# An expert layer's head: norm, turns and logits tile by tile, and its modulation rows loaded and combined one stage earlier

## The chip, the cores and the metric

One core of a Trainium2 chip runs the whole program, 68,690 instructions in a long row of stages. The metric is the device time of one execution in microseconds; the span of a profile runs from its first to its last instruction. The engines are TensorE (PE, with its weight loads PEld), VectorE (DVE), ScalarE (ACT), GpSimd (POOL) and SyncE (SP), which only issues DMAs.

## The reference, cut to what matters

Two transformer blocks, all in float32. The first block has two layers, each with a mixer and an expert layer. Of the first block:

```python
x = x + g1 * y
h = rms_norm(x, norm2_g[i]) * (1.0 + sc2) + sh2
x = x + g2 * expert_choice_ffn(h, moe_router[i], moe_w1[i], moe_w3[i], moe_w2[i])
if not last:
    ctx = ctx + cg1 * yc
    hc = rms_norm(ctx, norm2_g[i]) * (1.0 + csc2) + csh2
    ctx = ctx + cg2 * expert_choice_ffn(hc, moe_router[i], moe_w1[i], moe_w3[i], moe_w2[i])
```

`x` has 512 rows of 1024, `ctx` 256 rows. The shift `sh2`, the scale `sc2` and the gates `g1`, `g2` are rows of 1024 that come from a modulation of the condition (`mod_dram` in the kernel, six parts of 1024 for each of the two conditions). `expert_choice_ffn` computes a softmax over 16 experts from `h @ router`, lets each expert choose its 64 best rows of `x` (and 32 of `ctx`), and runs a gated network with weights of 3 x 4 MB for each expert.

## The kernel before, in words

Rows of `x` lie in SBUF as six tiles of 128 rows (four of `x`, two of `ctx`). The program is a row of stages; each (`Stage`, L29) has its own semaphores and a block in which every engine has its own list of instructions, written out by hand, and all engines meet at its end. No planner orders anything.

The last stage of each mixer is `add_gated` (L1624): `linear` (L412) multiplies the mixer's output with a 1024 x 1024 weight and adds it, times the gate, to `x`. The weight comes in four pieces of 256 columns and 1 MB, loaded by SP (L452) into a ring of 3 landing buffers in layer 0 and of 2 in layer 1. ScalarE makes the high part of a piece (L505) and of the rows tile by tile (L510), VectorE the low parts (L523, L530), TensorE does 24 matmuls a unit (one tile, 256 columns; L493), and VectorE multiplies with the gate and adds (L1636, L1637). Eight banks of accumulator let TensorE run ahead of VectorE by eight units. `linear` can already take a list `beside` of DMAs that GpSimd issues at the stage's start (L460).

The next stage is the expert layer, `mixture` (L1130). SP loads the gain row of the norm and, for one or two conditions, a scale and a shift row, each spread over 128 partitions (512 KB each; L1224 to L1227), then the router, then the first four quarters of expert weights (1 MB each). Meanwhile ScalarE squares and sums all tiles of `x` (L1382). VectorE waits for the rows, combines `(1 + scale) * norm gain` (L1450), waits for all sums, makes the mean (L1456), ScalarE the root (L1384), VectorE the inverse (L1458), and then the normed tile in two instructions (L1460, L1462). TensorE turns each tile with eight transposes (L1277), ScalarE copies the turned tile out (L1388), and SP stores the normed tile to DRAM for the later gathers (L1233). When all tiles are turned, TensorE does the logits, 8 float32 matmuls of 16 columns a tile (two records each in the profile, L1284). Then come the softmax, a ranking by rounds of eight on VectorE (L1475 to L1477), the gathers by indirect DMA, and the stream: 192 quarters of 1 MB go through four landing buffers, ScalarE's high part (L1364), VectorE's low part (L1426) and 12 matmuls each. A quarter beyond the fourth is loaded only when a low part has been made, and the first low part comes after the ranking on VectorE.

In layer 0 the expert layer has six tiles and two conditions, in layer 1 four tiles and one.

Of the kernel before, what the change touches and what calls it, by code (L numbers as in the profile page):

```python
# [13 lines left out]
P = 128  # L14
D = 1024
# [396 lines left out]
def linear(nc, h, K, w, jobs, RING=3, whole=None, low_from=None, beside=(), mod=None):  # L412
# [18 lines left out]
    with Stage(nc) as st:  # L431
# [84 lines left out]
        def _(dve):  # L516
# [18 lines left out]
            for c, piece in enumerate(pieces):  # L535
# [9 lines left out]
                lo_part(c + RING)  # L545

# [583 lines left out]
def mixture(nc, d, i, x, nt, mod_dram, cst):  # L1130
# [21 lines left out]
    with Stage(nc) as st:  # L1152
        land = [st.sb(f"w_quarter{c}", [P, QK, D]) for c in range(NL)]
# [3 lines left out]
        hid = st.sb("hidden", [P, D])  # L1157
        g2r = st.sb("row_gain", [R, D])
        shared = st.sb("gains_then_rows", [P, 4, D])
        gain, shift = shared[:, 0:2, :], shared[:, 2:4, :]  # L1160
        rows, ys = [shared[0:R, c, :] for c in range(2)], [shared[0:R, 2 + c, :] for c in range(2)]
        ng = hid
        rw = st.sb("router", [P, KD, E])
        ss, rs = (st.sb(n, [P, nt]) for n in ("sum_squares", "inverse_root"))
        junk = st.sb("squares", [P, D])
# [18 lines left out]
        consts = st.sem("gains_landed")  # L1184
        router_landed = st.sem("router_landed")
        g2_landed = st.sem("row_gain_landed")
        squared, mean_ready, root_ready = st.sem("squared"), st.sem("mean_ready"), st.sem("root_ready")
# [27 lines left out]
        def _(sp):  # L1215
# [8 lines left out]
            sp.dma_start(ng[:, :], d["norm2_g"][i].partition_broadcast(P)).then_inc(consts, 16)  # L1224
            for r in range(NROW):
                sp.dma_start(gain[:, r, :], mod_dram[r, 4 * D:5 * D].partition_broadcast(P)).then_inc(consts, 16)
                sp.dma_start(shift[:, r, :], mod_dram[r, 3 * D:4 * D].partition_broadcast(P)).then_inc(consts, 16)  # L1227
# [42 lines left out]
        def _(pe):  # L1270
            bank = (p3, py)
            for t in range(nt):
# [7 lines left out]
            pe.wait_ge(router_landed, 16)  # L1280
            for t in range(nt):
                pe.wait_ge(n_kept, 2 * t + 2)
                for k in range(KD):
                    mm = nc.tensor.matmul(pl[:, t, :], nT[:, k, t * P:(t + 1) * P], rw[:, k, :],  # L1284
                                          start=(k == 0), stop=(k == KD - 1), skip_group_check=True)
            mm.then_inc(scored, 1)
# [70 lines left out]
        def _(act):  # L1357
# [21 lines left out]
            for t in range(nt):  # L1379
                if t:  # L1380
                    act.wait_ge(squared, t)
                nc.scalar.activation(junk[:, :], x[:, t, :], ACT.Square, accum_out=ss[:, t:t + 1]).then_inc(squared, 1)  # L1382
            act.wait_ge(mean_ready, 1)
            nc.scalar.activation(rs[:, :], ss[:, :], ACT.Sqrt).then_inc(root_ready, 1)  # L1384
            for t in range(nt):
                for half in range(2):
# [3 lines left out]
                                         .rearrange("p (k r) -> p k r", k=HK), ACT.Copy).then_inc(n_kept, 1)  # L1390
            act.wait_ge(ready, 1)
# [25 lines left out]
        def _(dve):  # L1417
# [30 lines left out]
            dve.wait_ge(consts, 16 * (1 + 2 * NROW))  # L1448
            for r in range(NROW):
                last = nc.vector.scalar_tensor_tensor(out=gain[:, r, :], in0=gain[:, r, :], scalar=1.0, in1=ng[:, :],  # L1450
                                                      op0=ALU.add, op1=ALU.mult)
            chain(last)
            if RT > R:
                nc.vector.memset(hid[R:RT, :], 0.0)
            dve.wait_ge(squared, nt)
            nc.vector.tensor_scalar(ss[:, :], ss[:, :], 1.0 / D, EPS, ALU.mult, ALU.add).then_inc(mean_ready, 1)  # L1456
            dve.wait_ge(root_ready, 1)
            chain(nc.vector.reciprocal(rs[:, :], rs[:, :]))  # L1458
            for t in range(nt):
                chain(nc.vector.scalar_tensor_tensor(out=h[:, t, :], in0=x[:, t, :], scalar=rs[:, t:t + 1],  # L1460
# [871 lines left out]
NDR = 14  # L2332


def odd_layer(nc, d, x, modT, gates, gate_row, cst, ahead):

    ident = cst["ident"]
    RWI, NAD = 1920, 512
# [869 lines left out]
```

## Time and profile before

| | us |
|---|---|
| median of 3 runs (5191.65 to 5210.83) | 5204.43 |
| profiled execution | 5182.43 |
| its span | 5180.6 |
| PE busy | 4192.4 (81%) |
| DVE busy | 3071.3 (59%) |
| ACT busy | 1888.9 (36%) |
| mean granted TensorE clock | 0.879 of full speed |

The two expert layers are at 747 to about 1440 and at 2618 to about 3280 us of the span. In these stretches the core's 16 DMA engines move some 360 GB/s. A granted clock of 1.00 is 2.4 GHz, 0.50 is 1.2 GHz. In the timeline a row is one instruction or some merged ones: start, duration, engine, line, operation, output and input, and in brackets how long the engine sat idle before it and which instruction released it.

### The profile page before, as it was taken

To read this page: it belongs to the slowest core of one execution; us is meant where nothing else is said; L and a number is where in the kernel's file an instruction comes from. 1 tells how busy PE (TensorE), PEld (TensorE's weight loads), DVE (VectorE), ACT (ScalarE), POOL (GpSimd) and SP (SyncE) were. 2 spreads that over 40 slices of the span, in tenths; PEclk is the share of its full clock that TensorE was granted. 3 is DMA by queue.
4 is the path that set the end of the run, shared out by engine and by line. 5 is a ranking of instruction groups with operands and counts; after the bars stand their busy time and mean duration, and the time that the engine had idled before them with its cause. 6 is when DMAs were issued, how large, how long until landed. Compare 5 with 4: busy or idle time off the path is not lost. (4 is left out here: it accounts for less than half of the span.)

```text
span 5180.6 us, 68690 instructions
## 1 busy us (share of the span) xinstructions
PE 4192.4 (81%) x28028; PEld 3310.1 (64%) x28028; DVE 3071.3 (59%) x4349; ACT 1888.9 (36%) x2461; POOL 549.9 (11%) x419
## 2 busy tenths in 40 slices
PE   6868867999956887979669999686799856785998
PEld 2755665666656866869545555465687655674777
DVE  5259946888824556665458888436476234454672
ACT  4122324666622313222126666315322112352221
POOL 0111000111112003323001112002000001000000
PEclk9988787999978997978779999888899967897999
DMA  6120036999930220000249999400122201000322
GB/s 235 54 83 25 1 108 226 364 363 362 334 117 29 74 84 6 3 6 2 100 161 356 365 362 357 159 25 1 56 95 94 92 29 34 1 1 33 114 94 77
DMA packets 246407, 658.34 MB, mean 127 GB/s; under 512 B 27028, under 2 KB 91796, under 8 KB 245576
## 3 DMA queue, kind: packets, MB, share of 16 engines
q1 hardware_dynamic: 227808, 615.14, 33.3%
q0 software_dynamic: 8064, 30.46, 2.2%
q10 hardware_dynamic: 10224, 8.36, 0.5%
q8 instruction: 224, 3.67, 0.3%
q14 instruction: 87, 0.71, 0.0%
HBM read 624.97 MB, written 28.41 MB: 126 GB/s over the span
## 5 line engine op out<-in xcount | busy, mean ns | idle before, releaser
L1426 DVE TENSOR_TENSOR w_lo<-w_quarter,w_hi 128x2048 fp32r<-128x2048 f32 x384 | 874.0, 2287 | 200.0 <-ACT w_hi L1364 198.7
L1364 ACT ACTIVATE w_hi<-w_quarter 128x2048 fp32r<-128x2048 f32 x384 | 735.4, 1917 | 379.2 <-DMA w_quarter<-in_moe_w 188.3
L2682 DVE TENSOR_TENSOR w_lo<-w_chunks,w_hi 128x1024 fp32r<-128x1024 f32 x132 | 161.8, 1226 | 301.4 <-ACT w_hi L2660 301.4
L2634 PE MATMUL ffn_ps<-ffn_inT_hi,w_hi 128*128 128x512 f32 x704 | 276.4, 393 | 16.5 <-DVE w_lo L2682 16.5
L2634 PE MATMUL ffn_ps<-ffn_inT_lo,w_hi 128*128 128x512 f32 x704 | 275.9, 392 | 0.0
L2634 PE MATMUL ffn_ps<-ffn_inT_hi,w_lo 128*128 128x512 f32 x704 | 275.6, 391 | 0.0
L1265 POOL DMA_INDIRECT summed_dram<-gains_then_rows,row_token x32 | 137.9, 4310 | 1005.6 <-DVE gains_then_rows L1445 1005.6
L1312 PE MATMUL down_ps<-w_hi,hiddenT 128*96 128x512 f32 (+1 forms) x512 | 208.1, 406 | 39.2 <-DVE w_lo L1426 26.6
L900 PE MATMUL probT_ps<-ident,prob 128*128 128x128 f32 x896 | 164.6, 301 | 82.6 <-ACT prob L980 80.4
L967 ACT ACTIVATE probT<-probT_ps 128x256 f32<-128x256 f32 (+4 forms) x272 | 142.2, 523 | 223.5 <-PE probT_ps L900 223.5
L1312 PE MATMUL gate_ps<-w_hi,rowsT 128*96 128x512 f32 (+1 forms) x512 | 206.2, 403 | 12.5 <-DVE w_lo L1426 9.6
L1312 PE MATMUL up_ps<-w_hi,rowsT 128*96 128x512 f32 (+1 forms) x512 | 204.7, 400 | 7.4 <-DVE w_lo L1426 7.4
L2660 ACT ACTIVATE w_hi<-w_chunks 128x1024 fp32r<-128x1024 f32 x132 | 138.5, 1049 | 189.4 <-PE ffn_ps L2647 163.7
L1314 PE MATMUL gate_ps<-w_lo,rowsT 128*96 128x512 f32 (+1 forms) x512 | 204.4, 399 | 0.0
L1314 PE MATMUL down_ps<-w_lo,hiddenT 128*96 128x512 f32 (+1 forms) x512 | 204.2, 399 | 0.0
L1314 PE MATMUL up_ps<-w_lo,rowsT 128*96 128x512 f32 (+1 forms) x512 | 201.8, 394 | 0.0
L980 ACT ACTIVATE prob<-score_ps,negmax 128x256 f32<-128x256 f32 (+4 forms) x272 | 166.1, 611 | 87.2 <-DVE negmax L949 85.2
L588 PE MATMUL lin_ps<-w_hi,haT 128*128 128x512 f32 (+1 forms) x576 | 178.8, 391 | 23.3 <-DVE w_lo L612 23.3
L406 PE MATMUL turn_ps<-ident,normed 128*128 128x128 f32 x286 | 58.1, 377 | 166.1 <-DVE normed L363 153.5
L505 ACT ACTIVATE w_hi<-w_landing 128x2048 fp32r<-128x2048 f32 (+4 forms) x39 | 64.7, 1661 | 343.5 <-PE lin_ps L493 221.8
L900 PEld LDWEIGHTS probT_ps<-ident,prob 128*128 128x128 f32 x896 | 106.4, 150 | 126.2 <-ACT prob L980 118.3
L612 DVE TENSOR_TENSOR w_lo<-w_landing,w_hi 128x2048 fp32r<-128x2048 f32 (+2 forms) x28 | 56.2, 2007 | 184.4 <-ACT w_hi L602 184.4
(648 smaller groups left out, 10173.8 us busy)
## 6 DMA issues: line engine op xcount, KB each, us to landing
w_quarter<-in_moe_w SPq DMA_DIRECT2D x384, 1024.0 KB, 6.5
w_chunks<-in_f_w_up SPq DMA_DIRECT2D x88, 512.0 KB, 3.2
ada_landing<-in_ada_w SPq DMA_DIRECT2D x24, 1024.0 KB, 7.0
ada_ring<-in_ada_w SPq DMA_DIRECT2D x24, 1024.0 KB, 5.2
w_chunks<-in_f_w_down SPq DMA_DIRECT2D x44, 512.0 KB, 3.2
w_landing<-in_od_w_in SPq DMA_DIRECT2D x13, 1024.0 KB, 7.2
w_landing<-in_a_w_in SPq DMA_DIRECT2D x12, 1024.0 KB, 5.1
w_landing<-in_ev_w_in SPq DMA_DIRECT2D x6, 1024.0 KB, 7.4
```

The lines of the kernel that those rows point to most:

```text
L588: mm = nc.tensor.matmul(ps[n % 2][i][:, 0:width], h[:, g * HK + k, cols], v[:, c % NP, k, 0:width], start=(g + k + j == 0), stop=(g == 1 a ...
L900: mm = nc.tensor.transpose(tps(a, b), pr[:, i % SB, a:b], ident)
L967: nc.scalar.activation(pT[:, i % SB, 0:n], tps(0, n), ACT.Copy).then_inc(tkept, 1)
L980: nc.scalar.activation(pr[:, i % SB, 0:u[1]], score(i, 0, u[1]), ACT.Exp, bias=mx[:, m:m + 1], scale=scale, accum_out=sm[:, m:m + 1]).then ...
L1265: nc.gpsimd.indirect_dma_start(out=sum_dram, out_offset=bass.IndirectOffsetOnAxis(ap=idx[:, e:e + 1], axis=0), in_=ys[e % 2], in_offset=No ...
L1312: nc.tensor.matmul(out[0:R, cols], v[0][:, k, :], wh[c][:, kk, cols], start=first, stop=False, skip_group_check=True)
L1314: nc.tensor.matmul(out[0:R, cols], v[0][:, k, :], wl[c][:, kk, cols], start=False, stop=False, skip_group_check=True)
L1364: nc.scalar.activation(wh[g % NP][:, :, :], land[g % NL][:, :, :], ACT.Copy).then_inc(hi_ready, 1)
L1426: tt(wl[g % NP][:, :, :], land[g % NL][:, :, :], wh[g % NP][:, :, :].bitcast(F32), ALU.subtract) \
L2634: mm = nc.tensor.matmul(ps[c % 4][:, :], w[:, c % NP, cols], h[:, k, :], start=(k + i == 0), stop=(k == KD - 1 and i == 2))
L2660: nc.scalar.activation(wh[:, c % NP, :], land[:, c % NL, :], ACT.Copy).then_inc(hi_ready, 1)
L2682: nc.vector.tensor_tensor(wl[:, c % NP, :], land[:, c % NL, :], wh[:, c % NP, :].bitcast(F32), ALU.subtract).then_inc(split, 1)
```

## The change

`mixture` no longer loads and combines the rows. A new class `RowGains` holds them in SBUF, at a place that the stage before and the expert layer both leave free; `add_gated` passes its loads to `linear` as `beside` (GpSimd issues them) and its `combine` as `then`, which VectorE runs after the second weight piece's units. In layer 1 the ring of `linear` is 3 now, as in layer 0. In `mixture`, each tile has its own square, root, inverse and norm; the mean and the epsilon are folded into the root; the logits of tile t come on TensorE after the turn of tile t + 1. The landing buffers of the stream lie in another order in SBUF, around the rows.

```diff
-def linear(nc, h, K, w, jobs, RING=3, whole=None, low_from=None, beside=(), mod=None):
+def linear(nc, h, K, w, jobs, RING=3, whole=None, low_from=None, beside=(), mod=None, then=None):
...
                 lo_part(c + RING)
+                if c == 1 and then is not None:
+                    dve.wait_ge(beside_done, 16 * len(beside))
+                    then()
...
+class RowGains:
+    def __init__(self, nc, ctx, d, i, rows, mod_dram):
+        self.nc, self.rows = nc, rows
+        self.shared = ctx.enter_context(nc.sbuf_tensor(f"gains_then_rows_{Stage.turn}", [P, 4, D], F32))
+        self.hid = ctx.enter_context(nc.sbuf_tensor(f"gain_then_hidden_{Stage.turn}", [P, D], F32))
+        self.gain, self.shift = self.shared[:, 0:2, :], self.shared[:, 2:4, :]
+        self.loads = [(self.hid[:, :], d["norm2_g"][i].partition_broadcast(P))]
+        for r in range(rows):
+            self.loads.append((self.gain[:, r, :], mod_dram[r, 4 * D:5 * D].partition_broadcast(P)))
+            self.loads.append((self.shift[:, r, :], mod_dram[r, 3 * D:4 * D].partition_broadcast(P)))
+    def combine(self):
+        for r in range(self.rows):
+            self.nc.vector.scalar_tensor_tensor(out=self.gain[:, r, :], in0=self.gain[:, r, :], scalar=1.0,
+                                                in1=self.hid[:, :], op0=ALU.add, op1=ALU.mult)
...
-        land = [st.sb(f"w_quarter{c}", [P, QK, D]) for c in range(NL)]
+        land = [st.sb(f"w_quarter{c}", [P, QK, D]) for c in range(nt // 2)]
+        st.sb("gains_of_the_stage_before", [P, 5, D])
+        land += [st.sb(f"w_quarter{c}", [P, QK, D]) for c in range(nt // 2, NL)]
...
-            sp.dma_start(ng[:, :], d["norm2_g"][i].partition_broadcast(P)).then_inc(consts, 16)
-            for r in range(NROW):
-                sp.dma_start(gain[:, r, :], mod_dram[r, 4 * D:5 * D].partition_broadcast(P)).then_inc(consts, 16)
-                sp.dma_start(shift[:, r, :], mod_dram[r, 3 * D:4 * D].partition_broadcast(P)).then_inc(consts, 16)
...
+            def logits(t):
+                if t == 0:
+                    pe.wait_ge(router_landed, 16)
+                pe.wait_ge(n_kept, 2 * t + 2)
+                for k in range(KD):
+                    mm = nc.tensor.matmul(pl[:, t, :], nT[:, k, t * P:(t + 1) * P], rw[:, k, :],
+                                          start=(k == 0), stop=(k == KD - 1), skip_group_check=True)
+                return mm
...
-            pe.wait_ge(router_landed, 16)
-            for t in range(nt):
-                pe.wait_ge(n_kept, 2 * t + 2)
...
+                if t:
+                    logits(t - 1)
+            logits(nt - 1).then_inc(scored, 1)
...
-            for t in range(nt):
+            def root(t):
                 if t:
                     act.wait_ge(squared, t)
                 nc.scalar.activation(junk[:, :], x[:, t, :], ACT.Square, accum_out=ss[:, t:t + 1]).then_inc(squared, 1)
-            act.wait_ge(mean_ready, 1)
-            nc.scalar.activation(rs[:, :], ss[:, :], ACT.Sqrt).then_inc(root_ready, 1)
+                act.wait_ge(squared, t + 1)
+                nc.scalar.activation(rs[:, t:t + 1], ss[:, t:t + 1], ACT.Sqrt, bias=eps[:, :], scale=1.0 / D) \
+                    .then_inc(root_ready, 1)
+            act.wait_ge(eps_ready, 1)
+            for t in range(min(3, nt)):
+                root(t)
...
+                if t + 3 < nt:
+                    root(t + 3)
...
-            dve.wait_ge(consts, 16 * (1 + 2 * NROW))
-            for r in range(NROW):
-                last = nc.vector.scalar_tensor_tensor(out=gain[:, r, :], in0=gain[:, r, :], scalar=1.0, in1=ng[:, :],
-                                                      op0=ALU.add, op1=ALU.mult)
-            chain(last)
+            nc.vector.memset(eps[:, :], EPS).then_inc(eps_ready, 1)
...
-            dve.wait_ge(squared, nt)
-            nc.vector.tensor_scalar(ss[:, :], ss[:, :], 1.0 / D, EPS, ALU.mult, ALU.add).then_inc(mean_ready, 1)
-            dve.wait_ge(root_ready, 1)
-            chain(nc.vector.reciprocal(rs[:, :], rs[:, :]))
             for t in range(nt):
+                dve.wait_ge(root_ready, t + 1)
+                chain(nc.vector.reciprocal(rs[:, t:t + 1], rs[:, t:t + 1]))
...
+        gains = RowGains(nc, ctx, d, 0, 2, mod_dram)
+        add_gated(nc, catT, KD, d["ev_w_out"], x, list(range(NT)), lambda t: gates[:, 0 if t < LT else 1, :], gains.loads,
+                  gains.combine)
...
-        linear(nc, (hh, hl), K, w, [("tok", 0, D, tiles, keep)], RING=3 if n == TOK else 2, whole=inT)
+        linear(nc, (hh, hl), K, w, [("tok", 0, D, tiles, keep)], whole=inT, beside=beside, then=then)
...
+        ctx.close()
+        gains = RowGains(nc, outer, d, 1, 1, mod_dram)
+        add_gated(nc, catT, KD, d["od_w_out"], x, tiles[:LT], lambda t: gates[:, 0, :], gains.loads, gains.combine)
```

## Rows read from the trace of the kernel before

**Rows 1.** Windows: us, then each engine busy, PEclk, DMA share, GB/s; ranking, stream.
```profile
795.00:829.90 34.90, 3.30 (x16) 2.13 (x16) 31.27 (x74) 6.66 (x6) 3.88 (x3) 0.50 0.16 48
...
930.00:1030.00 100.00, 96.19 (x439) 66.80 (x437) 85.94 (x51) 67.79 (x46) 19.03 (x6) 1.00 1.01 362
```

**Rows 2.** Timeline of the first expert layer's head.
```profile
747.07 1.06 ACT L1382 ACTIVATE squares<-x 128x1024 f32<-128x1024 f32 x1 [51.10 <-PEq L67]
...
748.04 0.19 ACT L1382 ACTIVATION_READ_ACCUMULATOR squares<-x 128x1 f32 x1
...
754.14 1.28 ACT L1384 ACT_TABLE_LOAD   x1
757.82 2.36 DVE L1450 SCALAR_TENSOR_TENSOR gains_then_rows<-gains_then_rows,hidden 128x1024 f32<-128x1024 f32 x2 [11.10 <-DMA gains_then_rows<-mod_rows]
...
760.41 0.21 ACT L1384 ACTIVATE inverse_root<-sum_squares 128x6 f32<-128x6 f32 x1 [4.99 <-DVE sum_squares L1456]
760.65 0.19 DVE L1458 RECIPROCAL inverse_root<-inverse_root 128x6 f32<-128x6 f32 x1 [0.27 <-ACT inverse_root L1384]
760.88 1.28 DVE L1460 SCALAR_TENSOR_TENSOR normed_rows<-x,inverse_root,gains_then_rows 128x1024 f32<-128x1024 f32 x1
...
763.34 1.28 DVE L1460 SCALAR_TENSOR_TENSOR normed_rows<-x,inverse_root,gains_then_rows 128x1024 f32<-128x1024 f32 x1
...
763.48 1.97 PE L1277 MATMUL up_ps<-ident,normed_rows 128*128 128x128 f32 x8 [17.68 <-DVE normed_rows L1462]
...
777.51 17.39 PE L1284 MATMUL misc_ps<-router,normedT 128*128 128x16 f32 x96
...
794.94 0.26 DVE L1464 TENSOR_REDUCE row_max<-misc_ps 128x6 f32<-128x96 f32 x1 [19.24 <-PE misc_ps L1284]
```

**Rows 3.** Timeline of the second expert layer's head.
```profile
2618.08 1.06 ACT L1382 ACTIVATE squares<-x 128x1024 f32<-128x1024 f32 x1 [22.30 <-PEq L67]
...
2630.77 1.97 PE L1277 MATMUL up_ps<-ident,normed_rows 128*128 128x128 f32 x8 [13.97 <-DVE normed_rows L1462]
...
2639.89 13.68 PE L1284 MATMUL misc_ps<-router,normedT 128*128 128x16 f32 x64
```

**Rows 4.** Windows, PE alone: us, busy, PEclk, DMA share, GB/s; turns and logits.
```profile
768.30:769.50 1.20, 1.09 (x8) 1.00 1.00 406
...
777.50:780.00 2.50, 2.50 (x25) 0.98 0.97 231
...
2640.00:2642.00 2.00, 2.00 (x12) 0.50 0.91 307
```

**Rows 5.** Timeline: VectorE's keep in the stage ahead of the first expert layer.
```profile
742.96 0.42 DVE L1636 TENSOR_TENSOR gated<-lin_ps,gates 128x256 f32<-128x256 f32 x1 [2.00 <-PE lin_ps L493]
```

**Rows 6.** Timeline: the first weight piece of four stages, issue and first use.
```profile
663.77 10.09 SPq L452 DMA_DIRECT2D w_landing<-in_ev_w_out  x4
669.24 1.91 ACT L505 ACTIVATE w_hi<-w_landing 128x2048 fp32r<-128x2048 f32 x1 [11.68 <-DMA w_landing<-in_ev_w_out]
...
1485.12 18.72 SPq L452 DMA_DIRECT2D w_landing<-in_od_w_in  x4
...
1492.38 1.91 ACT L505 ACTIVATE w_hi<-w_landing 128x2048 fp32r<-128x2048 f32 x1 [13.38 <-DMA w_landing<-in_od_w_in]
...
1748.49 21.39 SPq L452 DMA_DIRECT2D w_landing<-in_od_w_in  x4
1749.09 4.32 POOL L459 DMA_DIRECT2D h1T_low_1b<-h1T_low  x8 [113.61 <-POOLq L67]
1755.17 1.91 ACT L505 ACTIVATE w_hi<-w_landing 128x2048 fp32r<-128x2048 f32 x1 [12.66 <-DMA w_landing<-in_od_w_in]
...
2557.72 16.67 SPq L452 DMA_DIRECT2D w_landing<-in_od_w_out  x4
...
2563.01 1.91 ACT L505 ACTIVATE w_hi<-w_landing 128x2048 fp32r<-128x2048 f32 x1 [8.63 <-DMA w_landing<-in_od_w_out]
```

**Rows 7.** DMA issues: line, engine, count, KB each, median us from issue to landing.
```profile
gates<-mod_rows POOLq DMA_DIRECT2D x2, 512.0 KB, 7.5
```

More of the change, by code:

```diff
@@ L1156, in mixture @@
         hT = [st.sb(f"hiddenT{c}", [P, KD, R], F32R) for c in range(2)]
-        hid = st.sb("hidden", [P, D])
+        hid, shared, gain, shift = gains.hid, gains.shared, gains.gain, gains.shift
         g2r = st.sb("row_gain", [R, D])
-        shared = st.sb("gains_then_rows", [P, 4, D])
-        gain, shift = shared[:, 0:2, :], shared[:, 2:4, :]
         rows, ys = [shared[0:R, c, :] for c in range(2)], [shared[0:R, 2 + c, :] for c in range(2)]
-        ng = hid
         rw = st.sb("router", [P, KD, E])
         ss, rs = (st.sb(n, [P, nt]) for n in ("sum_squares", "inverse_root"))
+        eps = st.sb("eps", [P, 1])
         junk = st.sb("squares", [P, D])
@@ L1519, with even_layer @@
 CONV = 512
-def even_layer(nc, d, x, modT, gates, cst, ahead, next_loads):
+def even_layer(nc, d, x, modT, gates, cst, mod_dram, ahead, next_loads):
     ident = cst["ident"]
@@ L1620, in even_layer, with add_gated @@
                       for ts in (range(LT), range(LT, NT)) for k in range(4)], ident)
-        add_gated(nc, catT, KD, d["ev_w_out"], x, list(range(NT)), lambda t: gates[:, 0 if t < LT else 1, :])
-def add_gated(nc, inT, K, w, x, tiles, gate):
+        gains = RowGains(nc, ctx, d, 0, 2, mod_dram)
+        add_gated(nc, catT, KD, d["ev_w_out"], x, list(range(NT)), lambda t: gates[:, 0 if t < LT else 1, :], gains.loads,
+                  gains.combine)
+        return gains
+def add_gated(nc, inT, K, w, x, tiles, gate, beside, then):
     n = inT.shape[2]
@@ L2332, with odd_layer @@
 NDR = 14
-def odd_layer(nc, d, x, modT, gates, gate_row, cst, ahead):
+def odd_layer(nc, d, x, modT, gates, cst, mod_dram, ahead):
     ident = cst["ident"]
@@ L2339, in odd_layer @@
     tiles = list(range(NT))
-    with ExitStack() as ctx:
+    with ExitStack() as outer, ExitStack() as ctx:
         def sb(name, shape, c=ctx):
             return c.enter_context(nc.sbuf_tensor(name, shape, F32))
-        catT = sb("mixedT_1", [P, KD, SEQ])
+        catT = sb("mixedT_1", [P, KD, SEQ], outer)
         gm = sb("gm1_1", [P, 2, KD])
@@ L2448, in odd_layer @@
             load_all(nc, [(gn[:, 0, :], d["gn_g"].partition_broadcast(P)), (gn[:, 1, :], d["gn_b"].partition_broadcast(P)),
[L2449 removed]
+                          (x[:, 0:LT, :], x_kept), (gates[:, 0, :], mod_dram[0, 2 * D:3 * D].partition_broadcast(P))], mod=mod)
             group_norm_gate(nc, Y, T, d, gn[:, 0, :], gn[:, 1, :], catT, ident, mod)
[L2451 removed]
+        ctx.close()
+        gains = RowGains(nc, outer, d, 1, 1, mod_dram)
+        add_gated(nc, catT, KD, d["od_w_out"], x, tiles[:LT], lambda t: gates[:, 0, :], gains.loads, gains.combine)
+        return gains
 F_TILES = 2816 // P
@@ L3104, in build @@
                        needed, loads)
-            even_layer(nc, d, x, modT[0], gates, cst, ahead, columns)
-            mixture(nc, d, 0, x, NT, mod_dram[0], cst)
+            gains = even_layer(nc, d, x, modT[0], gates, cst, mod_dram[0], ahead, columns)
+            mixture(nc, d, 0, x, NT, mod_dram[0], cst, gains)
         with nc.sbuf_tensor("gates1", [P, 1, D], F32) as gates:
-            odd_layer(nc, d, x, modT[1], gates, mod_dram[1][0, 2 * D:3 * D], cst, ahead)
-            mixture(nc, d, 1, x, LT, mod_dram[1], cst)
+            gains = odd_layer(nc, d, x, modT[1], gates, cst, mod_dram[1], ahead)
+            mixture(nc, d, 1, x, LT, mod_dram[1], cst, gains)
         forgetting(nc, d, x, cst)
```

12 lines of the change are left out of this document (3 added, 9 removed).

## The prediction

> **What bounds the kernel now.** I read first what is alike all over: in the stream of expert weights (windows by stage) TensorE is busy 96% of the time and the DMA engines are full [rows 1], so nothing outside that stream is worth anything unless it moves the stream's start. Then the head of each expert layer, which is the part that the change touches. It is a chain, and the timeline shows it as one [rows 2]: at 747.07 ScalarE squares six tiles, loads a table and is done at 755.42; VectorE meanwhile waits for the five row loads until 757.82, combines for 2.36 us, then scales the sums, waits for the root (until 760.62), inverts, and makes tile 0 between 760.88 and 763.48, where TensorE first moves. So the last wait to end ahead of tile 0 is that for the loads, and the squares of all tiles are behind it by 2.4 us. From 763.48 VectorE sets the pace (2.46 us a tile, the pitch from 760.88 to 763.34), TensorE turns each tile and waits. From 777.51 to 794.90 TensorE does the 96 matmuls of the logits alone, and VectorE starts again at 794.94, at once. What follows (softmax, ranking, gather, rows turned, 794.9 to 829.9) has VectorE busy for 31.3 of 34.9 us [rows 1]; none of it is touched, and the weight stream hangs on its end. The head of the second expert layer is the same with four tiles [rows 3]: 2618.08 to 2630.77 without TensorE, logits from 2639.89 to 2653.57.
>
> **Granted clock in the logits.** This decides the size [rows 4]. The clock is at 2.4 GHz (1.00) in the third tile's turn, where eight transposes take 1.09 us, and at 1.2 GHz (0.50) for most others, where they take 1.97 us. In the logits it is 0.98 for the first 2.5 us and 0.50 afterwards, though TensorE has no gap at all. In the second layer it is 0.50 already in the window from 2640 to 2642 (12 instructions in 2 us), right after a turn, and all 64 logit matmuls take 13.68 us [rows 3], 0.214 us each. [...]
>
> **The change part by part.**
>
> Start of tile 0, first layer. Removed from the path: the wait for the loads, 2.36 us of combining, five of six squares. Left: the memset of eps and ScalarE's wait for it (no such row; between 0 and 0.3 us, by the inverse, an instruction on six columns that is 0.23 us from start to start; I take 0.15), square and read 1.24, a self-wait 0.05, the table load 1.28, root 0.21, inverse until the product starts 0.26, product and sum until TensorE starts 2.60 (760.88 to 763.48) [rows 2]. 747.07 + 5.79 = 752.9: 10.6 us earlier. Second layer: the same without a table load (the function table is already the right one there, no such row stands in its head): 2618.08 + 4.5 = 2622.6 against 2630.77 [rows 3], 8.2 us earlier. VectorE's memset of the hidden rows lies beside ScalarE's square.
>
> The Trainium skill (ScalarE: Activation LUTs, "What ACT_TABLE_LOAD costs") gives such a load 1.28 us and a drain of about 1.4 us more. The load's own row agrees; the drain would be new on the path here, and by the page the gain below would be 1.4 us smaller.
>
> The tiles. VectorE now also inverts per tile: 2.46 + 0.23 (L1458's start to L1460's, 760.65 to 760.88) = 2.69 us a tile [rows 2]. ScalarE has per tile square, root and two copies, 1.24 + 0.05 + 0.21 + 1.2 = 2.7 us. TensorE has per tile a turn and 16 logit matmuls. At 1.2 GHz that is 1.97 + 16 x 0.214 = 5.39 us, twice VectorE's pace, so TensorE becomes the bound from tile 1 on. Order: turn 0, wait for tile 1, turn 1, logits 0, turn 2, ..., logits 5. First layer: tile 1 is ready at 752.9 + 2.69 = 755.6, then 5 x 1.97 + 6 x 3.42 = 30.4, end 786.0. Before 794.9: 8.9 us gained, less than the 10.6 of the start: from first turn to last logit TensorE needs 33.1 us at 1.2 GHz, and it needs 31.4 now, because the gaps of its turns are paid back by turns and logits that are in part at 2.4 GHz. Second layer: 2622.6 + 2.69 + 3 x 1.97 + 4 x 3.42 = 2644.9 against 2653.57: 8.7 us. Together 17.6. Ends: if no transposes and no logits lift the clock, this; if all of it ran at 2.4 GHz a tile would cost 1.09 + 16 x 0.107 (25 instructions stand in the first 2.5 us of the logits [rows 4]; I take 0.107) = 2.8 us, see the rivals.
>
> After the logits nothing changes. The table load for the exponential is issued after the last copy and hides under logits 5 (3.4 us) as it now hides under all of them. The stores of the normed tiles go out earlier; they must be in when the ranking is over, some 27 us after the logits. The DMA order in the SP queue: five loads fewer stand ahead of the router and the four weight quarters. Nobody waits for either in those 10 us but logits 0, for the router (64 KB), first needed at 757.6, ten microseconds after its issue, where a first piece of 1 MB takes five and a half [rows 6]. The eps bias costs an operand and no time that a row shows; below nothing is excluded, above I allow 0.1 us.
>
> The stage before (`linear` with `beside` and `then`). Moved there: five loads of 512 KB for layer 0 and three for layer 1, issued by GpSimd at the stage's start, and three combinations of 1.2 us on VectorE. The combinations come after the second of four weight pieces. TensorE needs 2.88 us a unit (VectorE's pair of 0.42 and 0.42 us and 2.00 idle [rows 5]), so VectorE has two thirds free, and eight units of accumulator lie between them: 2.4 us is hidden. If the loads were late there, VectorE would stand in front of the keeps, and TensorE would stop after 8 units, 23 us; the loads are by then 30 us old. The loads are not free. They meet the first weight piece, and on that hang its high part, its low part, the rows' split and TensorE's start, all in series. Piece 0 is used 5.47 us after its issue in this stage now (663.77 to 669.24) and 5.29 us in the second (2557.72 to 2563.01). The stages with loads beside them stand as nearest rows: 6.68 us with eight loads of 384 KB (1748.49 to 1755.17) and 7.26 us with two of 3 and 2 MB (1485.12 to 1492.38) [rows 6]. So 1.3 to 1.9 us more each; I take 1.5, nearer the row with many medium loads, 3.0 for both. Ends: 0 (GpSimd issues after SP), and, if piece 0 had to let all of it by at the 362 GB/s of the weight stream [rows 1], 2.6 MB + 1.6 MB = 7.2 + 4.3 = 11.5 us. Pieces 1 and 2 come later by up to 7 us, but are needed 17 us after piece 0. Ring 3 in place of 2 in the second layer puts one more low part (2.3 us) ahead of VectorE's first keep; the same eight units hide it, and TensorE had no gap between pieces there before, so it gains nothing either.
>
> The other buffer order in SBUF: 0, no row bears on it.
>
> Sum: 17.6 - 3.0 = 14.6 us. The profiled execution took 5182.4 us (span 5180.6 and 1.8 around it), that is 5167.8 after. The runs shown have a median of 5204.4, 22 us over that execution, and spread over 19 us; the same difference from the median gives 5189.8.
>
> **The rivals.**
>
> A. The clock goes up. TensorE has no gap from tile 1 on, and turns come among the logits. Then a tile costs 2.8 us, nearly VectorE's 2.69: first layer end 752.9 + 2.69 + 5 x 2.8 + 1.7 = 771.3 or so, 23.6 us gained, second 2622.6 + 2.69 + 3 x 2.8 + 1.7 = 2635.4, 18.2 gained, together 41.8 - 3.0 = 38.8: 5165.6. For it: two turns, 0.7 us apart, stand ahead of logits 0, and two came ahead of the third tile, the fast one [rows 4]. Against: 15 us of gapless logits at 0.50, and the window after the turn in the second layer. In part (one fast stretch a layer) it is worth some 2 to 4 us. The Trainium skill (TensorE: Matmul & The Clock Gate, "What's actually happening") has activity release the throttle; taken at its word the gapless stretch would be at 2.4 GHz, and this rival is what it gives. The logits of the trace go against it.
>
> B. The change does not pay in the start what it says: the overlap of squares, roots and copies on ScalarE makes tile after tile late (ScalarE at 2.7 us a tile and waits of both neighbours in it). Then TensorE waits at each tile. Price 1 to 1.5 us a tile, 10 to 15 us in all, result 0 to 5 us gained: 5202. Against: TensorE needs 5.4 us a tile, twice what ScalarE does.
>
> C. Slower: the GpSimd-issued row loads hold up the first weight piece. Two such loads, 1 MB, landed 7.5 us (median) after their issues where they met a stream [rows 7]; with 0.6 us between the issues that is 8.1 us, 130 GB/s. At that pace 2.6 MB take 20 us and 1.6 MB 12 us; if piece 0 stood behind them, TensorE would start 32 us late, and the result is 17.6 - 32 = 14 us slower, 5219. It turns to a loss from 17.6 us of delay in both stages together. For: TensorE's start has nothing ahead of it but this piece. Against: in the two nearest stages the piece was 1.3 and 1.9 us late only.
>
> **How the numbers follow.** Forecast 0.66, A 0.10 (in full or for the most part), B 0.14, C 0.05; 0.05 is left for what the spread does by itself. What a measurement of this kernel can tell from no change is about 0.5%, 26 us; the forecast lies inside. Faster by over 26 us needs A, or the forecast with a lucky median (the runs shown are up to 13 us off theirs): 0.19. Slower by over 26 us needs C at its worst and noise: 0.04. Within: 0.77. Range: from A's 5166, short of it by some, to B with noise: 5170 to 5210.
>
> **What would show it right or wrong.** TensorE's first transpose 5.8 us after the head's first square in layer 0 and 4.5 in layer 1; logits' end 38.9 and 26.8 us after that square (now 47.8 and 35.5); granted clock 0.50 there; the ranking part unchanged at 27 to 35 us; the first piece of the two stages before used 6.8 to 7 us after its issue; no wait of VectorE on the loads in it. The prediction is wrong if the clock in the logits is near 1.00, if TensorE waits between tiles for VectorE, or if the first piece is over 3 us late.

## The result, and the profile after

| kernel | median us (range, executions) | kernel before beside it | ratio, 95% interval |
|---|---|---|---|
| changed, first comparison | 5163.0 (5151.0 to 5191.0, 7) | 5203.2 (5184.4 to 5210.8, 7) | 0.9939 [0.9913, 0.9965] |
| changed, second comparison | 5166.8 (5161.9 to 5175.7, 6) | 5188.6 (5177.3 to 5211.0, 28) | 0.9963 [0.995, 0.9975] |

The change makes the kernel faster by some 0.4 to 0.6%: on either side of the 0.5% that the prediction took for its bound of no change. The forecast, 14.6 us off 5204.4, is a ratio of 0.9972: inside the second interval, just outside the first. As a time, 5189.8 was 27 and 23 us too high, and both medians lie under the range, by 7 and 3 us.

The profiled executions alone would tell the opposite: a span of 5180.6 us before and 5189.0 after. The unchanged recurrence of the second layer makes the difference. The rows are the timeline of SP, which loads a small matrix at the start of each of its two directions, and a window of the first direction (us; PE, PEld, DVE, ACT, POOL busy; clock, DMA share, GB/s); first the kernel before, then the changed one.

```profile
1950.83 0.35 SPq L2153 DMA_DIRECT2D w<-in_rw_w  x1
...
2220.61 0.33 SPq L2153 DMA_DIRECT2D w<-in_rw_w  x1
...
1951.00:2220.00 269.00, 233.70 (x4384) 212.06 (x4384) 160.13 (x302) 70.44 (x164) 88.63 (x90) 0.84 0.02 4
```
```profile
1950.73 0.35 SPq L2182 DMA_DIRECT2D w<-in_rw_w  x1
...
2237.39 0.33 SPq L2182 DMA_DIRECT2D w<-in_rw_w  x1
...
1951.00:2237.00 286.00, 250.46 (x4384) 228.79 (x4384) 160.43 (x303) 70.36 (x164) 88.65 (x90) 0.78 0.02 4
```

Start to start, the first direction took 269.8 us before and 286.7 after; in other profiles of the same two kernels it is the other way round, 283.9 before and 270.3 after. The swing goes with TensorE's granted clock: the same 4384 matmuls keep it busy for 233.7 us where the clock is 0.84 and for 250.5 us where it is 0.78, while VectorE, ScalarE and GpSimd are busy for the same time in both. So the kernel has to be read by stage, with times counted from where the change starts.

The head of the first expert layer in the changed kernel, timeline of all engines (start, duration, engine and line, operation, tiles; idle time before and what ended it in brackets), answering to [rows 2]:

```profile
749.61 1.06 ACT L1407 ACTIVATE squares<-x 128x1024 f32<-128x1024 f32 x1 [51.26 <-DVE eps L1480]
...
750.78 1.28 ACT L1409 ACT_TABLE_LOAD   x1
752.07 0.29 ACT L1409 ACTIVATE inverse_root<-sum_squares,eps 128x1 f32<-128x1 f32 x1
...
755.20 1.97 PE L1306 MATMUL up_ps<-ident,normed_rows 128*128 128x128 f32 x8 [7.03 <-DVE normed_rows L1488]
755.25 1.28 DVE L1486 SCALAR_TENSOR_TENSOR normed_rows<-x,inverse_root,gains_then_rows 128x1024 f32<-128x1024 f32 x1
...
757.85 1.97 PE L1306 MATMUL down_ps<-ident,normed_rows 128*128 128x128 f32 x8 [0.69 <-DVE normed_rows L1488]
757.91 1.29 DVE L1486 SCALAR_TENSOR_TENSOR normed_rows<-x,inverse_root,gains_then_rows 128x1024 f32<-128x1024 f32 x1
...
759.61 3.43 PE L1297 MATMUL misc_ps<-router,normedT 128*128 128x16 f32 x16
...
762.89 1.95 PE L1306 MATMUL up_ps<-ident,normed_rows 128*128 128x128 f32 x8
...
786.55 0.26 DVE L1490 TENSOR_REDUCE row_max<-misc_ps 128x6 f32<-128x96 f32 x1 [16.95 <-PE misc_ps L1297]
```

TensorE starts 5.6 us after the first square and has no gap from 759.61 until VectorE takes the logits 36.9 us after that square; before it was 16.4 and 47.9 us [rows 2]. The second layer, answering to [rows 3], and the granted clock of both stretches (windows: us, PE, PEld, DVE, ACT, POOL busy, clock, DMA share, GB/s):

```profile
2633.39 1.06 ACT L1407 ACTIVATE squares<-x 128x1024 f32<-128x1024 f32 x1 [33.98 <-DVE eps L1480]
...
2637.70 1.97 PE L1306 MATMUL up_ps<-ident,normed_rows 128*128 128x128 f32 x8 [5.75 <-DVE normed_rows L1488]
...
2659.03 0.22 DVE L1490 TENSOR_REDUCE row_max<-misc_ps 128x4 f32<-128x64 f32 x1 [13.42 <-PE misc_ps L1297]
```
```profile
766.00:786.00 20.00, 20.00 (x97) 20.00 (x97) 2.67 (x3) 5.66 (x10) 0.00 (x0) 0.50 0.68 264
2637.00:2659.00 22.00, 20.60 (x96) 20.09 (x96) 8.40 (x10) 7.85 (x15) 0.00 (x0) 0.50 0.94 370
```

The stage before, with the row loads in it (SP issues the weight pieces, GpSimd the rows), answering to [rows 6]; the second piece's high part is the fifth line, the combine the sixth:

```profile
666.44 12.21 SPq L453 DMA_DIRECT2D w_landing<-in_ev_w_out  x4
667.12 0.61 POOL L462 DMA_DIRECT2D gain_then_hidden<-in_norm_g  x1 [245.33 <-POOLq L67]
667.74 2.13 POOL L462 DMA_DIRECT2D gains_then_rows<-mod_rows  x4
671.67 1.91 ACT L506 ACTIVATE w_hi<-w_landing 128x2048 fp32r<-128x2048 f32 x1 [11.56 <-DMA w_landing<-in_ev_w_out]
682.17 1.92 ACT L506 ACTIVATE w_hi<-w_landing 128x2048 fp32r<-128x2048 f32 x1 [2.91 <-DMA w_landing<-in_ev_w_out]
...
714.45 2.35 DVE L1149 SCALAR_TENSOR_TENSOR gains_then_rows<-gains_then_rows,gain_then_hidden 128x1024 f32<-128x1024 f32 x2
...
2572.14 2.65 SPq L453 DMA_DIRECT2D w_landing<-in_od_w_out  x3
...
2577.55 1.91 ACT L506 ACTIVATE w_hi<-w_landing 128x2048 fp32r<-128x2048 f32 x1 [8.44 <-DMA w_landing<-in_od_w_out]
```

The first piece is used 5.23 and 5.41 us after its issue, against 5.47 and 5.29 before: no delay reaches it. The rows' bytes are paid by the second and third pieces. In layer 0 ScalarE takes them 15.7 and 19.7 us after the stage's first load and waits for both, where before it took them at 13.0 and 14.8 without a wait. TensorE shows no wait after its start, so this costs nothing.

**One table for all runs.** Each row is one profiled execution. "Linear" is from the first load of the residual stage to the head's first load; "head" from there to the release of the first buffer of the weight stream (its last instruction before that is VectorE's first low part); "to expert" from the same start to the first expert matmul. All in us, layer 0 / layer 1.

| kernel | linear | head | to expert |
|---|---|---|---|
| before | 83.3 / 60.3 | 77.6 / 58.6 | 82.9 / 67.7 |
| before, again (5203.6, one time) | 83.1 / 60.4 | 77.6 / 58.6 | 83.0 / 66.9 |
| changed | 83.0 / 61.1 | 66.5 / 48.9 | 76.0 / 57.3 |
| changed, again | 83.2 / 60.8 | 66.5 / 48.9 | 76.4 / 57.2 |
| logits_last | 83.9 / 60.5 | 70.7 / 51.0 | 80.1 / 59.5 |
| rows_early_only | 84.0 / 60.6 | 75.4 / 50.8 | 84.6 / 59.7 |
| rows_late | 83.5 / 59.7 | 76.5 / 56.3 | 85.9 / 64.6 |
| rows_sp_first | 92.9 / 65.0 | 66.5 / 48.9 | 76.0 / 57.8 |
| tile_moving | 83.2 / 60.1 | 56.8 / 44.3 | 66.1 / 53.0 |
| gather_first | 83.2 / 60.8 | 67.0 / 49.3 | 72.3 / 54.4 |
| tile_moving_gather_first | 83.2 / 59.9 | 57.3 / 44.7 | 62.7 / 49.8 |

The heads gain 11.1 and 9.7 us, 20.8 in all, more than the 17.6 forecast. But layer 0's expert matmuls start only 6.9 us earlier (82.9 to 76.0): 4.1 us are given back between the release of the stream and its first matmul. Layer 1 keeps 10.5 (9.7 against the other profile of before). Together that is 17.4 us (16.3 by the second profile of each kernel), and the two linear stages together cost 0.4 to 0.5. The weight streams add nothing: from the first expert matmul to the last scatter they take 604.0 and 608.1 us in the two profiles of before, 608.7 and 608.8 after (layer 1: 595.5 and 596.0, then 592.5 and 595.3).

### The profile page after: what moved, and what is told of

It is laid out like the page before. It is cut to its first block and busy times, and to the rows that moved or that the text cites. A ratio compares the mean times of both kernels' runs of the same rounds, so it can differ in the third digit from the quotient of the medians.

```text
span 5189.0 us, 68706 instructions
## 1 busy us (share of the span) xinstructions
PE 4220.5 (81%) x28028; PEld 3339.6 (64%) x28028; DVE 3075.9 (59%) x4357; ACT 1892.2 (36%) x2469; POOL 519.2 (10%) x427
## 5 line engine op out<-in xcount | busy, mean ns | idle before, releaser
L1337 PE MATMUL up_ps<-w_hi,rowsT 128*96 128x512 f32 (+1 forms) x512 | 204.4, 399 | 15.9 <-DVE w_lo L1458 15.8
L1284 POOL DMA_INDIRECT summed_dram<-gains_then_rows,row_token x32 | 105.3, 3291 | 1043.4 <-DVE gains_then_rows L1477 1043.4
```

Source lines behind the costliest of these rows:

```text
L1284: nc.gpsimd.indirect_dma_start(out=sum_dram, out_offset=bass.IndirectOffsetOnAxis(ap=idx[:, e:e + 1], axis=0), in_=ys[e % 2], in_offset=No ...
L1337: nc.tensor.matmul(out[0:R, cols], v[0][:, k, :], wh[c][:, kk, cols], start=first, stop=False, skip_group_check=True)
```

## The experiments

**The same kernel again, and its tile order taken back.** `after_again` is the changed kernel unedited:

> The changed kernel once more, nothing edited. In the two profiles so far the two expert heads (first SP instruction of the stage to the first released weight quarter) take 77.6 and 58.6 us before, 66.5 and 48.9 us after, 20.8 us less together; the medians of seven runs differ by 40 us. Theory 1 (the gain is in the heads alone, the rest is spread of stages that the change doesn't touch): the heads take 66.5 and 48.9 us again to 0.5 us, the weight streams and the stages between them differ from both profiles by up to 17 us with either sign, and the ratio comes out near 0.996 (20 us). Theory 2 (something beyond the heads is faster too, the streams for instance, which start earlier): the streams take clearly less than the 613 and 608 us of before, and the ratio stays at 0.994 or below.

It gave 0.9963, in agreement with theory 1, and the same heads to 0.1 us. `logits_last` leaves everything but the place of the logits:

```diff
-                if t:
-                    logits(t - 1)
+            for t in range(nt - 1):
+                logits(t)
             logits(nt - 1).then_inc(scored, 1)
```

> The changed kernel with the logits of all tiles after the turns of all tiles. Theory 1 (interleaving fills TensorE's gaps while the clock is at 1.2 GHz either way): turns at VectorE's pace of 2.66 us a tile, then 96 and 64 logit matmuls at 0.214 us; the heads are longer than in the changed kernel by 1.3 to 4.5 us (layer 0, less if the clock is at 2.4 GHz in the first logits as it was before) and 2.3 us (layer 1). Rival (interleaving is worth nothing, as the clock gives back the gaps): the heads equal those of the changed kernel to 0.5 us.

Measured 5178.5 us (5171.4 to 5202.6, 10), ratio 0.9992 [0.9976, 1.0008]; the heads are 4.2 and 2.1 us longer. Its TensorE has one turn per 2.65 us, waiting 0.69 us before each, and then all logits in one row:

```profile
772.57 20.50 PE L1297 MATMUL misc_ps<-router,normedT 128*128 128x16 f32 x96
```

So the logits between the turns fill TensorE's waits, and are worth 6.3 us of the heads' 20.8.

**The two halves of the change alone.** `rows_early_only` has the rows loaded and combined in the stage before, but squares, root and logits as before (one root after all squares, logits after all turns). `rows_late` has the new tile order, with the rows loaded and combined in the head again:

```diff
+            for to, src in gains.loads:
+                sp.dma_start(to, src).then_inc(consts, 16)
             sp.dma_start(rw[:, :, :], d["moe_router"][i]
...
+            dve.wait_ge(consts, 16 * len(gains.loads))
+            for r in range(gains.rows):
+                last = nc.vector.scalar_tensor_tensor(out=gain[:, r, :], in0=gain[:, r, :], scalar=1.0,
+                                                      in1=hid[:, :], op0=ALU.add, op1=ALU.mult)
```

> The rows are loaded and combined in the stage before, but the head squares all tiles, makes one mean and one root, turns all tiles, then does all logits, as before. Theory 1: the head now waits for the squares, done 4.8 us (layer 0, 755.4 against 760.2) and 4.7 us (layer 1) before the combination was; the heads take 72.8 and 53.9 us, 9.5 us less together, ratio 0.998. Rival (early rows are worth nothing without the tile order, or cost the stage before 3 us as predicted): heads as said, but the two stages before longer by 1.5 us each.

> Tile by tile norms and logits between the turns as in the changed kernel, but the rows are loaded by SP at the head's start and combined there as before. Theory 1: the tile order alone gains next to nothing, since tile 0 waits for the combination again: TensorE's first turn 0.5 to 1 us earlier than before, heads 76 to 77 and 57 us. Rival (the order of turns and logits is what gains): heads 72 or less and 55 or less.

Measured: `rows_early_only` 5185.6 us (5167.6 to 5206.6, 10), ratio 0.9997 [0.998, 1.0015], heads 75.4 and 50.8; `rows_late` 5185.3 us (5176.2 to 5197.9, 10), ratio 0.9996 [0.9981, 1.0011], heads 76.5 and 56.3. Neither half alone moves the time by what can be measured, though in the heads they are worth 10.0 and 3.4 us of the 20.8; the other 7.4 come only with both. The heads show why: with the loads in the path the tile order gains only 1.1 and 2.3 us, since tile 0 waits for the loads whatever the squares do (first turn 764.54, 15.6 us after its first square at 748.94); with the loads out of the way but six squares ahead of tile 0, the head gains 2.2 and 7.8 us. The last two numbers were expected at 4.8 and 4.7. The logits of `rows_early_only` in TensorE's timeline, and windows of it in layer 1 (us, PE busy, clock, DMA share, GB/s), show what came between:

```profile
775.68 20.50 PE L1296 MATMUL misc_ps<-router,normedT 128*128 128x16 f32 x96
...
2635.31 10.80 PE L1296 MATMUL misc_ps<-router,normedT 128*128 128x16 f32 x64
```
```profile
2635.30:2640.00 4.70, 4.70 (x39) 0.83 1.01 385
2640.00:2646.00 6.00, 6.00 (x29) 0.50 0.47 193
```

The same 96 matmuls took 17.39 us in the kernel before [rows 2] and take 20.50 here, and the 64 of layer 1 took 13.68 [rows 3] and take 10.80. In layer 1 the clock is still up for most of the first 4.7 us of the logits; in layer 0 all of them run at 0.50. How long the clock stays up behind the turns is worth 3 us, and it was lost in one layer and won in the other.

**Who issues the row loads.** `rows_sp_first` has SP issue them ahead of its weight pieces:

```diff
+            if then is not None:
+                for dst, src in beside:
+                    sp.dma_start(dst, src).then_inc(beside_done, 16)
             for c, (job, a, b) in enumerate(pieces):
```

> The changed kernel, but SP issues the row loads of the stage before, ahead of the weight pieces, instead of GpSimd. The changed kernel's first piece was used 5.2 and 5.4 us after its issue, no later than without the rows, where 6.8 to 7 was predicted. Theory 1 (GpSimd's issue comes so late that piece 0 is through; the second piece pays): here the first piece is used 12 us (layer 0) and 9 us (layer 1) after the stage's start, TensorE starts 6 and 4 us later, and the stages take that much longer. Rival (the DMA engines have room for both): first piece at most 2 us later.

Measured in a single execution: 5184.1 us. The linear stages are 9.9 and 3.9 us longer than in the changed kernel, where 6 and 4 were expected; the timeline of layer 0's:

```profile
669.15 0.35 SPq L452 DMA_DIRECT2D gain_then_hidden<-in_norm_g  x1
...
683.34 1.91 ACT L509 ACTIVATE w_hi<-w_landing 128x2048 fp32r<-128x2048 f32 x1 [20.20 <-DMA w_landing<-in_ev_w_out]
```

The piece is used 14.2 us after the stage's first load in place of 5.2. The 2.6 MB of rows that the changed kernel gets for nothing cost 9 us when they stand ahead of the piece. The two stages together lose 13.8 us, more than the 7.2 + 4.3 us that the prediction set as its upper end for contention. The edit changes the order and the issuing engine at once, and which of them counts is not shown.

**The clock in the logits.** `tile_moving` exchanges the operands of the logits, so that a matmul has 128 columns in place of 16. ScalarE copies the 16 x 128 result out, and TensorE turns it back at the end (six or four more matmuls):

```diff
-                    mm = nc.tensor.matmul(pl[:, t, :], nT[:, k, t * P:(t + 1) * P], rw[:, k, :],
+                    mm = nc.tensor.matmul(lb[t % 2][0:E, 0:P], rw[:, k, :], nT[:, k, t * P:(t + 1) * P],
...
+                return nc.tensor.transpose(pl[:, t, :], left[:, t * P:(t + 1) * P], ident[0:E, 0:E])
```

> The changed kernel, but in the logits the turned tile is the moving operand (128 columns) and the router the stationary one (16 columns); ScalarE copies the 16 x 128 result out and TensorE turns it back, six and four small transposes more. Theory 1 (logit matmuls with 16 columns keep the granted clock at 0.50, those with 128 lift it): granted clock over 0.8 in most of the logits, a tile's logits 1.7 to 2 us instead of 3.4; the heads shorter by 4 to 8 us (layer 0) and 2 to 5 us (layer 1) net of the turning back. Rival (the clock is down for another reason, the short gaps or the float32 passes): clock 0.50, a tile's logits 3.4 us as now, the heads 2 to 3 us longer.

Measured 5153.9 us (5146.7 to 5183.7, 9), ratio 0.9926 [0.9903, 0.995]. TensorE's timeline in layer 0, and a window of all engines:

```profile
759.62 3.48 PE L1301 MATMUL misc_ps<-normedT,router 128*16 128x128 f32 x16
763.03 1.10 PE L1314 MATMUL up_ps<-ident,normed_rows 128*128 128x128 f32 x8
764.06 1.92 PE L1301 MATMUL gate_ps<-normedT,router 128*16 128x128 f32 x16
```
```profile
766.00:786.00 20.00, 11.76 (x100) 9.41 (x100) 9.75 (x23) 11.62 (x17) 0.00 (x0) 0.85 0.68 262
```

At 0.50 a tile's logits cost the same in both forms (3.43 and 3.48 us). But with 128 columns the granted clock is up in the very next turn (1.10 us at 763.03, where the changed kernel's turn at 762.89 takes 1.95), and from there a turn takes 1.09 us and the logits 1.92: 2.87 us a tile in place of 5.01. The heads fall by another 9.7 and 4.6 us (4 to 8 and 2 to 5 were expected). Layer 1 and both layers of `tile_moving_gather_first` below show the same: the clock is at 1.00 from the third turn to the end of the logits. With 16 columns it is 0.50 from the first turn to the last logit in both layers of the changed kernel, of its second profile, of `gather_first` and of `rows_sp_first`, although TensorE is busy for all 20 us of the changed kernel's window. Where the clock was up at the start of 16-column logits, right behind turns, it fell while they ran without a gap (at the start of layer 0's logits before [rows 4], in layer 1 of `rows_early_only`). The exchange changes the moving and the stationary operand at once; which of the two the clock goes with is not shown. The Trainium skill (TensorE: Matmul & The Clock Gate, "What's actually happening") has activity release the throttle. Taken at its word, a TensorE that is busy without a gap would be at 1.00; the changed kernel's 20 us at 0.50 go against it, and the measurement decides.

**The 4 us given back.** After the ranking VectorE casts the row tokens; GpSimd issues the first gather with them, and VectorE goes on with the low parts of the weights. The timeline of the kernel before, layer 0 and then layer 1:

```profile
822.26 1.03 POOL L1249 DMA_INDIRECT gains_then_rows<-normed_dram,row_token  x1 [402.30 <-DVE row_token L1484]
822.26 6.72 DVE L1426 TENSOR_TENSOR w_lo<-w_quarter,w_hi 128x2048 fp32r<-128x2048 f32 x3 [0.29 <-DVE row_token L1484]
...
826.45 1.51 PE L1300 MATMUL misc_ps<-ident,gains_then_rows 96*128 96x96 f32 x8 [4.77 <-DMA gains_then_rows<-normed_dram,row_token]
...
829.98 0.74 PE L1312 MATMUL gate_ps<-w_hi,rowsT 128*96 128x512 f32 x1 [2.02 <-DVE rowsT L1433]
...
2674.36 6.69 DVE L1426 TENSOR_TENSOR w_lo<-w_quarter,w_hi 128x2048 fp32r<-128x2048 f32 x3
2674.61 2.90 POOL L1249 DMA_INDIRECT gains_then_rows<-normed_dram,row_token  x1 [202.50 <-DVE row_token L1484]
...
2683.78 1.08 PE L1300 MATMUL misc_ps<-ident,gains_then_rows 64*128 64x64 f32 x8 [9.74 <-DMA gains_then_rows<-normed_dram,row_token]
```

and of the changed kernel, layer 0:

```profile
813.62 6.70 DVE L1458 TENSOR_TENSOR w_lo<-w_quarter,w_hi 128x2048 fp32r<-128x2048 f32 x3
813.87 2.92 POOL L1268 DMA_INDIRECT gains_then_rows<-normed_dram,row_token  x1 [144.00 <-DVE row_token L1510]
815.94 19.67 SPq L1244 DMA_DIRECT2D w_quarter<-in_moe_w  x4
817.09 1.85 POOL L1268 DMA_INDIRECT gains_then_rows<-normed_dram,row_token  x1 [0.30 <-issue]
...
822.75 1.51 PE L1325 MATMUL misc_ps<-ident,gains_then_rows 96*128 96x96 f32 x8 [9.47 <-DMA gains_then_rows<-normed_dram,row_token]
...
825.44 0.74 PE L1337 MATMUL gate_ps<-w_hi,rowsT 128*96 128x512 f32 x1 [1.17 <-DVE rowsT L1465]
```

Where the low part starts with the gather, the gather takes 1.03 us and its rows are turned 4.2 us after its start. Where the low part is 0.25 us ahead, the gather takes 2.9 us and its rows are turned 8.9 us after. In both profiles of before, layer 0 is of the first kind; in every other kernel without the edit below, and in layer 1 of all of these, it is the second. `gather_first` gives VectorE three tiny instructions ahead of the low part:

```diff
+            for _ in range(3):
+                chain(nc.vector.memset(ss[:, :], 0.0))
             dve.wait_ge(h_stored, 16 * nt)
```

> The changed kernel with three short memsets of `ss` ahead of the wait after which VectorE makes its first low part, in both expert layers, so that GpSimd's first gather is issued before that low part starts. Theory 1 (GpSimd's issue is slowed by a VectorE low part that is already running): the gather's issue takes about 1.0 us again in place of 2.9, the turn of the gathered rows starts about 4.5 to 5 us behind the cast of the row tokens in place of 8.7, and the first expert matmul about 8 us in place of 11.6 to 12.2, so head start to first expert matmul is near 72.5 us in layer 0 (76.0 in the changed kernel) and each layer's stream is 2.5 to 4 us shorter: 6 us or so off the time, ratio near 0.995 to 0.996 against the kernel before becomes 0.994 to 0.995. Theory 2 (the slow issue goes with the place of the gather or the state of its queue, not with VectorE): the issue stays at 2.9 us, the first matmul at 11.6 us or more, and the memsets cost up to 0.3 us.

> The same three memsets on top of the form in which the normed rows are the moving operand of the logits. Theory 1: the gather's issue is about 1.0 us, the first expert matmul some 3.6 us earlier than in tile_moving in layer 0 and about 3 in layer 1, heads unchanged at 56.8 and 44.3 us, time near 5147 us against 5153.9, ratio near 0.991. Theory 2: the stages and the time are those of tile_moving.

`gather_first` measured 5158.3 us (5145.5 to 5183.0, 12) against 5191.8 (17 executions), ratio 0.9939 [0.9919, 0.996]. Its timeline in layer 0 and in layer 1:

```profile
813.19 0.33 DVE L1514 MEMSET sum_squares<- 128x6 f32 x3
813.41 1.00 POOL L1268 DMA_INDIRECT gains_then_rows<-normed_dram,row_token  x1 [144.21 <-DVE row_token L1510]
813.61 6.70 DVE L1458 TENSOR_TENSOR w_lo<-w_quarter,w_hi 128x2048 fp32r<-128x2048 f32 x3
...
817.83 1.51 PE L1325 MATMUL misc_ps<-ident,gains_then_rows 96*128 96x96 f32 x8 [5.00 <-DMA gains_then_rows<-normed_dram,row_token]
...
821.30 0.74 PE L1337 MATMUL gate_ps<-w_hi,rowsT 128*96 128x512 f32 x1 [1.96 <-DVE rowsT L1465]
...
2642.34 0.98 POOL L1268 DMA_INDIRECT gains_then_rows<-normed_dram,row_token  x1 [105.33 <-DVE row_token L1510]
...
2646.28 1.09 PE L1325 MATMUL misc_ps<-ident,gains_then_rows 64*128 64x64 f32 x8 [4.51 <-DMA gains_then_rows<-normed_dram,row_token]
```

The gather takes 1.0 us again, in both layers, and the first expert matmul comes 3.7 and 2.9 us earlier, although VectorE starts its low part 0.45 us later. The rival (the slow issue belongs to the gather's place or queue) falls: nothing about the gather was changed. The two overlap in both cases; what counts is which starts first. In time the gain is within the noise: 0.9939 here against 0.9963 and 0.9939 for the changed kernel.

How long the gather takes can be read from all eleven profiles. 329 gathers in them start while a low part runs, with 0.1 to 2.1 us of it left. Each takes what is left of that low part and 0.78 to 0.90 us more: the changed kernel's first gather has 2.04 left and takes 2.92, its second (817.09) has 1.02 left and takes 1.85. A low part that starts during a gather adds nothing (1.0 us, as above). So the gather takes as long as if it stood still until the running low part is over. 16 gathers start while VectorE makes the low part of the turned rows (`rowsT`, one input in the accumulator) with 0.12 to 0.35 us of it left; these take 0.90 to 0.92, no more than a gather alone (0.92 to 1.03). The Trainium skill (GPSIMD Engine Reference, "1. Specifications") says that GpSimd shares its SBUF interfaces with VectorE and contends with VectorE instructions of two SBUF inputs; the low part is one, `rowsT` is not, and the rows agree with both. The length of the wait is from the rows.

The gather's rows come 4.7 us later, not 1.9. The rows above suggest why: the slow gather ends at 816.79, behind the weight load that SP issued at 815.94 when the low part was done, and 1 MB at 362 GB/s [rows 1] is 2.9 us (an estimate). In `gather_first` the gather ends at 814.41, ahead of that load. This part was not tested by itself.

`tile_moving_gather_first`, with both edits, is the best version: 5141.9 us (5131.0 to 5144.2, 6), ratio 0.9903 [0.9875, 0.9931], first expert matmul 20.3 and about 17.6 us earlier than before (by the table, layer 1 against the mean of the two profiles).

## Why the prediction was right, and where it was off

- **What bounds the head: right.** Loads and squares ahead of tile 0 were the path. Either taken away alone gains nothing that the time shows (`rows_late`, `rows_early_only`).
- **Start of tile 0: right.** Predicted 5.8 and 4.5 us from the first square to the first turn, measured 5.59 and 4.31. The table load ends at 752.06 and the root starts at 752.07. The Trainium skill (ScalarE: Activation LUTs, "What ACT_TABLE_LOAD costs") adds a drain of about 1.4 us to such a load; the trace doesn't show one here.
- **VectorE's pace: right.** Predicted 2.69 us a tile, measured 2.66 (755.25 to 757.91).
- **TensorE's tile: right bound, size off.** Predicted 5.39 us, measured 5.01 (the same turn-and-logits step repeats from 762.89 to 767.90). The term that was mis-sized is the turn: 1.97 us is one turn from its first start to its last end, and between neighbours on a busy TensorE it takes 5.01 - 3.42 = 1.59. The prediction put 5 and 3 turns at 1.97, so that is 5 x 0.38 = 1.9 us in layer 0 and 1.1 in layer 1. Logits' end: predicted 38.9 and 26.8 us after the first square, measured 36.9 and 25.6.
- **The clock: right.** 0.50 in both heads from the first turn to the last logit; rival A did not come. Its clock came only with an edit that the change does not contain, and gave 9.7 + 4.6 = 14.3 us of the 24.2 that A set over the forecast.
- **Contention in the stage before: wrong.** Predicted 1.5 us each from the nearest rows, 3.0 in all; the piece came 0.2 us earlier and 0.1 later. The lower end that it gave, 0, is what happened for the first piece, and its reason (GpSimd issues after SP) fits `rows_sp_first`, which doesn't separate order from issuing engine; "pieces 1 and 2 later by up to 7 us" was right (2.8 and 4.9); the two nearest rows [rows 6] had the loads in other queue positions or sizes. The linear stages changed by -0.3 to +0.7 us. Rival C's price is real for another order: 9.9 and 3.9 us.
- **Rival B: wrong.** No wait of TensorE stands between tiles after the second turn.
- **"After the logits nothing changes": wrong.** Up to the cast of the row tokens it holds: VectorE takes 27.0 us from reading the logits in layer 0, before and after. The step fails at the first gather of layer 0, where a race of 0.25 us between two engines that no one orders costs 4.1 us. The row of before that would have told of it is layer 1's own gather, 2.90 us against 1.03, which the prediction did not compare. Why VectorE's first low part starts with the gather in layer 0 of before and 0.25 us ahead of it everywhere else stays open; the edits around it touch nothing that the low part waits for in plain sight.
- **The sum.** 17.6 - 3.0 = 14.6 predicted. By the table, the second profile of each kernel gives 6.6 + 9.7 - 0.5 = 15.8 us and the first 6.9 + 10.5 - 0.4 = 17.0 ("to expert" in both layers, less the linear stages). The turn (3.0 us) and the contention (3.0) were each set too dear, and the gather took 4.1 of it back. The ratios of whole times say 32 us (18 to 45) and 19 us (13 to 26). The second agrees with the stages; the first lies 15 us over them, which a swing of 17 us with the clock in a stage that the change does not touch could do, but that was not isolated. That the stages agree so well with 14.6 is in part luck: two terms set too dear stand against one that was missing.
- **The time itself** hangs on which median of before the 14.6 us are taken from: three runs gave 5204.4, the medians beside the changed kernel are 5203.2 (7) and 5188.6 (28). From 5188.6 the forecast would be 5174.0, 7 us over what was measured beside it. From 5203.2 it would be 5188.6, 26 us over, and the stages that the change touches don't show these. The range should have held a swing of 15 us in the kernel before.

## What to carry to other kernels

Two things that one tile waits for have to be moved together: here the halves alone gave 10.0 and 3.4 us of the heads' 20.8, and nothing that the time showed. When a stage ends earlier, compare the first instruction of the next stage, not the release of its first buffer: an unordered pair of engines there can take the gain back. And for a small matmul that repeats, try the long side as the moving operand: here it cost the same at 0.50, and in all four heads that had it the clock went to 1.00.

## What the runs showed of the hardware

- Transposes and 128-column logit matmuls, 24 instructions a tile, ran at 2.4 GHz (1.00) from the third turn on in four heads of two kernels; transposes between 16-column matmuls stayed at 1.2 GHz for 27 us with TensorE at 100% busy. Per instruction at 0.50: 0.214 us with 16 columns and 0.218 with 128; at the high clock 0.12 with 128.
- An indirect gather issued by GpSimd takes 0.9 to 1.0 us alone. If a VectorE `tensor_tensor` with two SBUF inputs is running when it starts, it takes the rest of that instruction and 0.78 to 0.90 us more (329 gathers), so 2.9 us if the first low part (2.29 us) started 0.25 us before it; its rows are then in use 8.3 to 9.2 us after its start in place of 3.9 to 4.4.
- Five loads of 512 KB issued by GpSimd from 0.7 us after SP's first 1 MB cost that piece nothing (5.2 us to use, against 5.5 without them) and the next two 2.8 and 4.9 us; issued by SP ahead of it they cost it 9 us.
- One unchanged stage took 270 or 284 to 287 us in four profiles, with the granted clock at 0.84 or at 0.78 to 0.79.
